# Attention stage: the small group of a projection tile moved in front of the value products, a large one between the turns, the gating product moved to their middle

## The chip, the cores and the metric

The kernel runs as one program on one core of a Trainium2 chip. The metric is the time of one execution on the device in microseconds (us), lower is better. The engines of the core are PE (TensorE, with its weight loads shown as PEld), DVE (VectorE), ACT (ScalarE), POOL (GpSimd) and SP (SyncE, which here only issues transfers).

## The reference, cut to what matters

One encoder layer over 1280 tokens (a prompt of 256 and a sample of 1024), width 1024. The part that the change touches:

```
xn = rms_norm(x, norm_mix_g)
q, k, v, gu, gv, z, xbc, dt, gates = split(xn @ w_in)
# A: banded attention, blocks of 128 queries against 3 x 128 keys, 8 heads
scores = qn @ kn.T + bias;  pr = exp(scores - m) / denom;  y_a = pr @ v
# B: chunked gating over 128 positions, 4 groups
vn = layer_norm(gelu(gv));  sv = w_spatial @ vn + b;  y_b = gelu(gu) * sv
```

After it come the state space branch (C), the merge of the three branches with the output projection, and the feed-forward part.

## The kernel before

Everything is held transposed, features on the 128 partitions and tokens along the free axis. The program has stages with a barrier between them: `project`, `attention_and_gmlp`, `state_space`, `merge` with the feed-forward part. The order on each engine is written out by hand, and engines wait for each other on counting semaphores.

`attention_and_gmlp` works on 10 chunks of 128 tokens. In each of its 10 steps (`step`, chunks 0 to 9) it does for its chunk the attention values and the gating branch, for the next chunk the scores, and beside them one tile of the late part of the input projection, which fills TensorE's time. Such a tile (`LateTiles`, name `la`) is 128 output features by 1280 tokens, in three token groups with an index g of 0 to 2. A group is 8 x 3 matmuls (`three_products`, L155 to L157: each weight and each activation is split into a high and a low half). Their widths come from

```
GROUPS = ((0, 512), (512, 512), (1024, 256))
```

so a group is "large" (512 tokens) or "small" (256). The accumulators alternate between two banks of `la_acc`; `read_out` on ScalarE (L780) copies each to `la_result`, with SiLU in chunks 0 to 5 and plainly in chunks 6 to 9, and the tile is stored from SP's queue (L742).

In a step TensorE's order is: `scores` of the next chunk (four pairs of L974 into two banks of `ps_scores`, two slices of group 0 behind each pair); `turn_v` (L1020, the gating branch's values are transposed); group 1 in one piece; `values`: eight turns (L985, three 128 x 128 transposes of the probabilities each, into two banks of `ps_turned`), which ScalarE copies out (L1161, `probs_T`), and four `products` (L994) of two heads each, with two slices of group 2 ahead of each product; at the end `mix` (L1026, the gating product of 4 x 128 columns).

ScalarE's order in a step is: `high_half` of a weight tile (L195), `gm_sum` (L1170), `read_out` of group 0, `gm_square` (L1174), `gm_root` (L1179, a square root), `read_out` of group 1, `results` (8 x L1161, then L1166), `read_out` of group 2, `exponents` of the next chunk (L1153). Before SiLU, the square root and the exponential the compiler puts an ACT_TABLE_LOAD, where the table before was another's.

VectorE's order is: `add_bias` (L1064, empties `ps_scores`), `low_half` (L200), `gm_mean`, `divide` (L1090 gives the probabilities, one operation a head), `gm_inverse` (L1101), `maxima` of the next chunk, `gm_normal` (L1106, gives `vn`, for which `mix` waits), `gm_gate` (L1113, L1116, which wait for `mix`). Turn i waits for probability i and, from the third on, for the copy of the turn two before it.

Of the kernel before, what the change touches and what calls it, by code (L numbers as in the profile page):

```python
# [25 lines left out]
HEADS, HD = 8, 64  # L26
# [32 lines left out]
GROUPS = ((0, 512), (512, 512), (1024, 256))  # L59
# [658 lines left out]
class LateTiles:  # L718
# [1 line left out]

    def __init__(self, ctx, nc, sem, name, ws, scratch, xn, first):
        def sb(what, shape):
            return ctx.enter_context(nc.sbuf_tensor(f"{name}_{what}", shape, F32))

        self.ws, self.result = ws, sb("result", [P, 2, T])
        self.acc = ctx.enter_context(nc.psum_tensor(f"{name}_acc", [P, 2, 512], F32))
        self.out = scratch["late_T"]
        self.xn, self.first = xn, first  # L730
        self.stored = [sem(f"{name}_stored{s}") for s in range(2)]
        self.full, self.read = (sem(f"{name}_{w}") for w in ("full", "read"))

# [26 lines left out]

    def product(self, pe, s, m, g, ks=range(KD)):

        t0, n = GROUPS[g]
        if 0 in ks:
            if g == 0:
                pe.wait_ge(self.ws.split_done, m + (B_LATE + self.first + 1))
            if not (isinstance(m, int) and 3 * m + g < 2):
                pe.wait_ge(self.read, m * 3 + (g - 1))
        for k in ks:
            mm = three_products(pe, self.acc[:, (s + g) % 2, 0:n], self.ws.hi[:, s, k], self.ws.lo[:, s, k],  # L770
                                self.xn[0][:, k, t0:t0 + n], self.xn[1][:, k, t0:t0 + n], k == 0, k == KD - 1)
        if KD - 1 in ks:
            mm.then_inc(self.full, 1)

    def read_out(self, act, s, m, g, func=ACT.Identity):
        t0, n = GROUPS[g]
        if g == 0 and not (isinstance(m, int) and m < 2):
            act.wait_ge(self.stored[s], m * 8 - 8 * s)
        act.wait_ge(self.full, m * 3 + (g + 1))
        act.activation(self.result[:, s, t0:t0 + n], self.acc[:, (s + g) % 2, 0:n], func).then_inc(self.read, 1)  # L780
# [66 lines left out]
def attention_and_gmlp(nc, a, scratch, consts, ws, xn, bias, sem):  # L847
# [9 lines left out]
    with ExitStack() as ctx:  # L857
# [19 lines left out]
        waste = sb("gm_waste", [P, E])  # L877
        gm_stat = sb("gm_stat", [P, 2, 4])
        y = sb("gm_y", [P, 2, G, P])
        late = LateTiles(ctx, nc, sem, "la", ws, scratch, xn, 0)  # L880
        ps_s = ctx.enter_context(nc.psum_tensor("ps_scores", [P, 2, 512], F32))
        ps_t = ctx.enter_context(nc.psum_tensor("ps_turned", [P, 2, 512], F32))
        ps_o = ctx.enter_context(nc.psum_tensor("ps_out", [P, 512], F32))
# [19 lines left out]
        with nc.Block() as block:  # L903
# [60 lines left out]
            @block.tensor  # L964
            def _(pe):
                def scores(s, chunk, loads, between=lambda h: None):

                    pe.wait_ge(qk_in[s], loads)
                    for j in range(HEADS // 2):
                        if not (first(chunk) and j == 0):  # L970
                            pe.wait_ge(s_read, chunk * 8 + 2 * j)
                        for g in range(2):
                            rows_of = slice(g * HD, (g + 1) * HD)
                            pe.matmul(ps_s[:, g, 0:W], q[rows_of, s, j, :], k[rows_of, s, :],  # L974
                                      start=True, stop=True).then_inc(s_full, 1)
                        between(2 * j)
                        between(2 * j + 1)

                def values(s, chunk, loads, between):
                    def turn(i):  # L980
                        pe.wait_ge(p_ready, chunk * 8 + (i + 1))
                        if not (first(chunk) and i < 2):
                            pe.wait_ge(t_read, chunk * 8 + (i - 1))
                        for b in range(3):
                            mm = pe.transpose(ps_t[:, i % 2, b * P:(b + 1) * P], S[:, s, ORDER[i], b * P:(b + 1) * P],  # L985
                                              masks[:, IDENT])
                        mm.then_inc(t_full, 1)

                    def products(j):

                        pe.wait_ge(t_read, chunk * 8 + (2 * j + 2))
                        for b in range(3):
                            for g in range(2):
                                mm = pe.matmul(ps_o[g * HD:(g + 1) * HD, j * P:(j + 1) * P],  # L994
                                               v[:, s, b, g * HD:(g + 1) * HD], PT[:, (2 * j + g) % 4, b],
                                               start=b == 0, stop=b == 2)
                        return mm

                    turn(0)
                    turn(1)  # L1000
                    pe.wait_ge(v_in[s], loads)
                    if not first(chunk):
                        pe.wait_ge(o_read, chunk)
                    for j in range(HEADS // 2):
                        if j + 1 < HEADS // 2:
                            turn(2 * j + 2)
                            turn(2 * j + 3)
                        between(2 * j)
                        between(2 * j + 1)
                        mm = products(j)  # L1010
                    mm.then_inc(o_full, 1)

                def turn_v(s, chunk, loads):
                    pe.wait_ge(uv_in[s], loads)
                    if first(chunk):
                        pe.wait_ge(shift_ok, 1)
                    else:
                        pe.wait_ge(scaled, chunk * 4)
                    for j in range(G):
                        mm = pe.transpose(ps_g[:, j * P:(j + 1) * P], uv[:, s, G + j], masks[:, IDENT])  # L1020
                    mm.then_inc(turned, 1)

                def mix(s, chunk):
                    pe.wait_ge(vn, chunk + 1)
                    for g in range(G):
                        mm = pe.matmul(ps_g[:, g * P:(g + 1) * P], vt[:, s, g * P:(g + 1) * P], w_sT[:, g],  # L1026
                                       start=True, stop=True)
                    mm.then_inc(mixed, 1)

                def step(s, chunk, loads, ahead):  # L1030

                    if ahead is not None:
                        scores(1 - s, chunk + 1, ahead, lambda h: late.product(pe, s, chunk + 2, 0, [h]))
                    else:
                        late.product(pe, s, chunk + 2, 0)
                    turn_v(s, chunk, loads)
                    late.product(pe, s, chunk + 2, 1)
                    values(s, chunk, loads, lambda h: late.product(pe, s, chunk + 2, 2, [h]))
                    mix(s, chunk)

                late.product(pe, 0, 0, 0)
                scores(0, 0, 48)
                pe.wait_ge(small_in, 64)
                for g in range(G):
                    mm = pe.matmul(ps_g[:, g * P:(g + 1) * P], ln_b[:, g * P:(g + 1) * P], w_sT[:, g], start=True, stop=True)
                mm.then_inc(shifted, 1)
                for m, g in ((0, 1), (0, 2), (1, 0), (1, 1), (1, 2)):
                    late.product(pe, m, m, g)
                step(0, 0, 16, 48)
                step(1, 1, 16, 96)  # L1050
                with pe.Fori(1, NT // 2 - 1) as pair:
                    step(0, pair * 2, pair * 16 + 16, pair * 48 + 48)
                    step(1, pair * 2 + 1, pair * 16 + 16, pair * 48 + 96)
                step(0, NT - 2, 16 * NT // 2, 48 * NT // 2)
                step(1, NT - 1, 16 * NT // 2, None)
# [93 lines left out]
            def _(act):  # L1149
# [4 lines left out]
                                       accum_out=stat[:, s, 2, h:h + 1]).then_inc(exp_done, 1)  # L1154
                    act.activation(stat[:, s, 1], stat[:, s, 1], ACT.Exp).then_inc(exp_done, 1)

                def results(s, chunk, stores):
                    for h in range(HEADS):

                        act.wait_ge(t_full, chunk * 8 + (h + 1))  # L1160
                        act.activation(PT[:, h % 4].rearrange("p b q -> p (b q)"), ps_t[:, h % 2, 0:W],  # L1161
                                       ACT.Identity).then_inc(t_read, 1)
                    act.wait_ge(o_full, chunk + 1)
                    if stores is not None:
                        act.wait_ge(o_stored[s], stores)
                    act.activation(out[:, s].rearrange("p j q -> p (j q)"), ps_o[:], ACT.Identity).then_inc(o_read, 1)  # L1166
# [14 lines left out]
                def step(s, chunk, stores, more=True, func=ACT.Silu):  # L1181
# [3 lines left out]
                    late.read_out(act, s, chunk + 2, 0, func)  # L1185
                    gm_square(s, chunk)
                    gm_root(s, chunk)
                    late.read_out(act, s, chunk + 2, 1, func)
                    results(s, chunk, stores)
                    late.read_out(act, s, chunk + 2, 2, func)  # L1190
                    if more:
                        exponents(1 - s, chunk + 1)
# [919 lines left out]
```

## Time and profile before

| | us |
|---|---|
| median of three runs | 2490.12 (2489.49 to 2491.94) |
| the profiled execution, its own time | 2490.52 |
| its span, first to last instruction | 2488.7 |
| TensorE busy in the span | 2367.1 |
| attention stage, from its first to its last matmul | 476.92 to 793.0 |

The span is 1.8 us shorter than the profiled execution's own time; that is what lies around it. Busy time of TensorE is the sum of its matmuls, whose ends are modelled. A row of the timeline begins with the start and the duration; in square brackets stands how long the engine was idle ahead of it, and what ended that. The granted clock (PEclk) is a share of TensorE's full clock of 2.4 GHz: 1.00 is 2.4 GHz and 0.50 is 1.2 GHz.

### The profile page before, as it was taken

To read this page: it belongs to the slowest core of one execution; us is meant where nothing else is said; L and a number is where in the kernel's file an instruction comes from. 1 tells how busy PE (TensorE), PEld (TensorE's weight loads), DVE (VectorE), ACT (ScalarE), POOL (GpSimd) and SP (SyncE) were. 2 spreads that over 40 slices of the span, in tenths; PEclk is the share of its full clock that TensorE was granted. 3 is DMA by queue.
4 is the path that set the end of the run, shared out by engine and by line. 5 is a ranking of instruction groups with operands and counts; after the bars stand their busy time and mean duration, and the time that the engine had idled before them with its cause. 6 is when DMAs were issued, how large, how long until landed. Compare 5 with 4: busy or idle time off the path is not lost.

```text
span 2488.7 us, 33412 instructions
## 1 busy us (share of the span) xinstructions
PE 2367.1 (95%) x13062; PEld 1970.9 (79%) x13062; DVE 1103.9 (44%) x1581; ACT 857.8 (34%) x1543; POOL 155.5 (6%) x72
## 2 busy tenths in 40 slices
PE   3999999699998999999799999999999999999999
PEld 1778888576777888888678888788888888888887
DVE  4310265336553666677555453533333333333333
ACT  4331223246654544566544131421121212111120
POOL 3333343000000000000000000000000000000000
PEclk8999999899999999999899999999999999999999
DMA  3122223422233666788574341111111111111112
GB/s 121 39 85 76 78 89 124 139 93 94 93 105 112 185 199 200 236 242 250 173 260 137 96 155 38 35 35 43 35 42 34 42 34 42 34 42 34 42 34 93
DMA packets 171003, 251.09 MB, mean 101 GB/s; under 512 B 10883, under 2 KB 125827, under 8 KB 168236
## 3 DMA queue, kind: packets, MB, share of 16 engines
q1 hardware_dynamic: 170924, 250.01, 31.8%
q8 instruction: 53, 0.87, 0.1%
q14 instruction: 26, 0.21, 0.0%
HBM read 189.57 MB, written 62.50 MB: 101 GB/s over the span
## 4 chain that ended last, share of the span: by engine, by line
PE 49%; DVE 1%; DMA 0%; SPq 0%; ACT 0%; issue 0%; DVEq 0%
PE acc L155 16%; PE acc L156 16%; PE acc L157 16%; DVE r_lo L1672 1%; DMA merged<-s_y_T 0%; PE acc L1929 0%; SPq L1709 0%; ACT r_hi L1662 0%; DVE h_T L1880 0%; DVE r_lo L1670 0%; ACT gates L1854 0%; DVE sums L1793 0%; DVE sums L1867 0%; DVE merged L1796 0%; DVE h_T L2036 0%
## 5 line engine op out<-in xcount | busy, mean ns | idle before, releaser
L155 PE MATMUL acc<-r_hi,w_hi 128*128 128x512 f32 (+1 forms) x1344 | 478.2, 356 | 17.1 <-DVE r_lo L1670 17.1
L156 PE MATMUL acc<-r_hi,w_lo 128*128 128x512 f32 (+1 forms) x1344 | 477.3, 355 | 0.0
L157 PE MATMUL acc<-r_lo,w_hi 128*128 128x512 f32 (+1 forms) x1344 | 476.5, 355 | 0.0
L155 PEld LDWEIGHTS acc<-r_hi,w_hi 128*128 128x128 f32 x1344 | 255.2, 190 | 54.8 <-issue 14.4
L156 PEld LDWEIGHTS acc<-r_hi,w_lo 128*128 128x128 f32 x1344 | 255.2, 190 | 35.3
L157 PEld LDWEIGHTS acc<-r_lo,w_hi 128*128 128x128 f32 x1344 | 254.8, 190 | 35.7
L156 PE MATMUL acc<-u_hi,w_lo 128*128 128x512 f32 (+1 forms) x768 | 273.6, 356 | 0.0
L155 PE MATMUL acc<-u_hi,w_hi 128*128 128x512 f32 (+1 forms) x768 | 273.6, 356 | 0.0
L157 PE MATMUL acc<-u_lo,w_hi 128*128 128x512 f32 (+1 forms) x768 | 273.6, 356 | 0.0
L195 ACT ACTIVATE w_hi<-w_raw 128x1024 fp32r<-128x1024 f32 x119 | 124.9, 1050 | 386.2 <-PE acc L157 380.1
L155 PE MATMUL acc<-xn_hi,w_hi 128*128 128x512 f32 (+1 forms) x624 | 225.2, 361 | 13.5 <-DVE xn_lo L317 8.7
L2036 DVE TENSOR_TENSOR h_T<-h_T,acc 128x512 f32<-128x512 f32 (+1 forms) x192 | 114.9, 598 | 264.8 <-PE acc L157 264.8
L156 PE MATMUL acc<-xn_hi,w_lo 128*128 128x512 f32 (+1 forms) x624 | 223.0, 357 | 0.0
L157 PE MATMUL acc<-xn_lo,w_hi 128*128 128x512 f32 (+1 forms) x624 | 222.5, 357 | 0.0
L200 DVE TENSOR_TENSOR w_lo<-w_raw,w_hi 128x1024 fp32r<-128x1024 f32 x119 | 145.5, 1223 | 99.0 <-ACT w_hi L195 98.9
L155 PE MATMUL s_l_acc<-xn_hi,w_hi 128*128 128x512 f32 (+1 forms) x480 | 179.8, 375 | 8.0 <-PEq L111 6.1
L157 PE MATMUL s_l_acc<-xn_lo,w_hi 128*128 128x512 f32 (+1 forms) x480 | 172.2, 359 | 0.0
L156 PE MATMUL s_l_acc<-xn_hi,w_lo 128*128 128x512 f32 (+1 forms) x480 | 171.7, 358 | 0.0
L155 PEld LDWEIGHTS acc<-u_hi,w_hi 128*128 128x128 f32 x768 | 144.1, 188 | 23.5
L156 PEld LDWEIGHTS acc<-u_hi,w_lo 128*128 128x128 f32 x768 | 144.1, 188 | 23.5
L157 PEld LDWEIGHTS acc<-u_lo,w_hi 128*128 128x128 f32 x768 | 144.1, 188 | 23.4
L1994 ACT ACTIVATE u_hi<-gates 128x512 fp32r<-128x512 f32 (+1 forms) x96 | 54.0, 562 | 312.8 <-DVE gates L2024 312.8
(204 smaller groups left out, 3458.0 us busy)
## 6 DMA issues: line engine op xcount, KB each, us to landing
w_raw<-in_w_tiles SPq DMA_DIRECT2D x146, 512.0 KB, 3.7
c_w<-s_ac SPq DMA_DIRECT2D x20, 1024.0 KB, 4.6
c_xbc<-s_xbc_T SPq DMA_DIRECT2D x20, 768.0 KB, 4.7
s_late_T<-s_l_result SPq DMA_DIRECT2D x20, 640.0 KB, 6.9
c_grown<-s_grown SPq DMA_DIRECT2D x40, 256.0 KB, 6.0
gates<-s_late_T SPq DMA_DIRECT2D x16, 512.0 KB, 3.8
s_xbc_T<-x_T_sb SPq DMA_DIRECT2D x12, 640.0 KB, 3.2
s_late_T<-la_result SPq DMA_DIRECT2D x12, 640.0 KB, 3.6
```

What stands on the lines that cost most here:

```text
L155: pe.matmul(out, w_hi, x_hi, start=first, stop=False)
L156: pe.matmul(out, w_lo, x_hi, start=False, stop=False)
L157: return pe.matmul(out, w_hi, x_lo, start=False, stop=last)
L195: act.activation(self.hi[:, s], self.raw[:, s], ACT.Identity).then_inc(self.hi_done, 1)
L200: dve.tensor_tensor(self.lo[:, s], self.raw[:, s], self.hi[:, s].bitcast(F32), ALU.subtract).then_inc(self.split_done, 1)
L1672: dve.scalar_tensor_tensor(low, src, self.gain[:, k:k + 1], high.bitcast(F32), ALU.mult, ALU.subtract).then_inc(self.low, 1)
L1994: act.activation(self.u_hi[:, i, t0:t0 + n], self.relu[:, u % 2, 0:n], ACT.Square).then_inc(self.high, 1)
L2036: dve.tensor_tensor(hh, hh, self.acc2[:, g, 0:n], ALU.add).then_inc(self.added, 1)
```

## The change

The tiles of this stage get their groups in another order: large, small, large. Group 1, which runs in one piece in front of the values, is the small one now, and group 2, which is spread between the turns, is a large one. `mix` moves from the end of the step to behind the second product of the values. On ScalarE `read_out` of group 1 moves from in front of the eight copies to their middle. The stage of the state space branch keeps the old order of groups for its own tiles. Nothing is added or taken away.

```
-    def __init__(self, ctx, nc, sem, name, ws, scratch, xn, first):
+    def __init__(self, ctx, nc, sem, name, ws, scratch, xn, first, groups=GROUPS):
...
-        t0, n = GROUPS[g]
+        t0, n = self.groups[g]
...
-        late = LateTiles(ctx, nc, sem, "la", ws, scratch, xn, 0)
+        late = LateTiles(ctx, nc, sem, "la", ws, scratch, xn, 0, (GROUPS[0], GROUPS[2], GROUPS[1]))
...
                         between(2 * j)
                         between(2 * j + 1)
                         mm = products(j)
+                        if j == 1:
+                            middle()
...
-                    values(s, chunk, loads, lambda h: late.product(pe, s, chunk + 2, 2, [h]))
-                    mix(s, chunk)
+                    values(s, chunk, loads, lambda h: late.product(pe, s, chunk + 2, 2, [h]), lambda: mix(s, chunk))
...
                     for h in range(HEADS):
-
+                        if h == HEADS // 2:
+                            middle()
...
-                    late.read_out(act, s, chunk + 2, 1, func)
-                    results(s, chunk, stores)
+                    results(s, chunk, stores, lambda: late.read_out(act, s, chunk + 2, 1, func))
```

The order of TensorE's instructions around the first turns of chunk 0, before. These are the end of group 1, the first four turns (`ps_turned`), the first slices of group 2 and the first product:

```order
L157 MATMUL la_acc<-xn_lo,w_hi 128x512
L985 MATMUL ps_turned<-masks_sb,scores_sb 128x128 x12
L155 MATMUL la_acc<-xn_hi,w_hi 128x256
L156 MATMUL la_acc<-xn_hi,w_lo 128x256
L157 MATMUL la_acc<-xn_lo,w_hi 128x256
```

The same place now:

```order
L157 MATMUL la_acc<-xn_lo,w_hi 128x256
L985 MATMUL ps_turned<-masks_sb,scores_sb 128x128 x12
L155 MATMUL la_acc<-xn_hi,w_hi 128x512
L156 MATMUL la_acc<-xn_hi,w_lo 128x512
L157 MATMUL la_acc<-xn_lo,w_hi 128x512
```

The group ahead of the turns is the narrow one now, and the slices behind them are wide.

The end of chunk 0's step on TensorE before, from the last slices of group 2 to the first scores of the next step:

```order
L155 MATMUL la_acc<-xn_hi,w_hi 128x256
L156 MATMUL la_acc<-xn_hi,w_lo 128x256
L157 MATMUL la_acc<-xn_lo,w_hi 128x256
L994 MATMUL ps_out<-probs_T,v_sb 64x128 x6
L1026 MATMUL ps_gmlp<-w_sT,v_turned_sb 128x128 x4
L974 MATMUL ps_scores<-k_sb,q_sb 128x384 x2
```

Now `mix` (L1028 in the new numbering, `ps_gmlp`) stands in the middle of the values, behind the second product and ahead of the last turns:

```order
L994 MATMUL ps_out<-probs_T,v_sb 64x128 x6
L1028 MATMUL ps_gmlp<-w_sT,v_turned_sb 128x128 x4
L985 MATMUL ps_turned<-masks_sb,scores_sb 128x128 x6
L155 MATMUL la_acc<-xn_hi,w_hi 128x512
L156 MATMUL la_acc<-xn_hi,w_lo 128x512
L157 MATMUL la_acc<-xn_lo,w_hi 128x512
```

The step now ends with a product, and the next scores follow it at once.

ScalarE in chunk 1's step before, from the load of SiLU's table for group 0 to the end of the step:

```order
L780 ACT_TABLE_LOAD
L780 ACTIVATE la_result<-la_acc 128x512
L1174 ACTIVATE gm_waste,gm_stat<-v_turned_sb,gm_stat 128x512
L1179 ACT_TABLE_LOAD
L1179 ACTIVATE gm_stat<-gm_stat 128x1
L780 ACT_TABLE_LOAD
L780 ACTIVATE la_result<-la_acc 128x512
L1161 ACTIVATE probs_T<-ps_turned 128x384 x8
L1166 ACTIVATE attn_out<-ps_out 128x512
L780 ACTIVATE la_result<-la_acc 128x256
```

And now, from the square root on:

```order
L1181 ACT_TABLE_LOAD
L1181 ACTIVATE gm_stat<-gm_stat 128x1
L1163 ACTIVATE probs_T<-ps_turned 128x384 x4
L780 ACT_TABLE_LOAD
L780 ACTIVATE la_result<-la_acc 128x256
L1163 ACTIVATE probs_T<-ps_turned 128x384 x4
L1168 ACTIVATE attn_out<-ps_out 128x512
L780 ACTIVATE la_result<-la_acc 128x512
```

The copies of the turns (`probs_T`) begin right behind the square root, and the table load with the copy of group 1 comes after four of them. The number of table loads is the same.

## Rows read from the trace of the kernel before

**Rows 1.** The page, busy time of each engine and share of the span.
```profile
PE 2367.1 (95%) x13062; PEld 1970.9 (79%) x13062; DVE 1103.9 (44%) x1581; ACT 857.8 (34%) x1543; POOL 155.5 (6%) x72
```

**Rows 2.** What TensorE waited for from 540 to 775: us, times, longest.
```profile
PE ps_turned L985 <- ACT probs_T L1161: 7.2, 8, 1.1
PE ps_scores L974 <- DVE scores_sb L1064: 4.0, 8, 0.5
```

**Rows 3.** Timeline of TensorE in chunk 3's step.
```profile
604.63 0.92 PE L974 MATMUL ps_scores<-k_sb,q_sb 64*128 64x384 f32 x4
...
607.68 0.92 PE L974 MATMUL ps_scores<-k_sb,q_sb 64*128 64x384 f32 x4 [0.55 <-DVE scores_sb L1064]
...
615.23 0.48 PE L155 MATMUL la_acc<-xn_hi,w_hi 128*128 128x512 f32 x1
...
620.80 0.82 PE L985 MATMUL ps_turned<-masks_sb,scores_sb 128*128 128x128 f32 x6
622.76 0.91 PE L985 MATMUL ps_turned<-masks_sb,scores_sb 128*128 128x128 f32 x6 [1.14 <-ACT probs_T L1161]
...
631.47 1.16 PE L1026 MATMUL ps_gmlp<-w_sT,v_turned_sb 128*128 128x128 f32 x8
632.56 0.92 PE L974 MATMUL ps_scores<-k_sb,q_sb 64*128 64x384 f32 x4
```

**Rows 4.** Timeline of ScalarE in chunk 3's step.
```profile
615.51 0.60 ACT L1170 ACTIVATE v_turned_sb<-ps_gmlp 128x512 f32<-128x512 f32 x1 [3.62 <-PE ps_gmlp L1020]
...
620.12 0.20 ACT L1179 ACTIVATE gm_stat<-gm_stat 128x1 f32<-128x1 f32 x1
...
622.13 0.87 ACT L1161 ACTIVATE probs_T<-ps_turned 128x384 f32<-128x384 f32 x2
```

**Rows 5.** Timeline of TensorE, small group of tile 1, first scores of chunk 0's step.
```profile
519.05 0.28 PE L155 MATMUL la_acc<-xn_hi,w_hi 128*128 128x256 f32 x1
...
522.02 0.92 PE L974 MATMUL ps_scores<-k_sb,q_sb 64*128 64x384 f32 x4
...
524.45 0.92 PE L974 MATMUL ps_scores<-k_sb,q_sb 64*128 64x384 f32 x4
```

**Rows 6.** Timeline of VectorE in chunk 3's step.
```profile
604.84 1.13 DVE L1113 SCALAR_TENSOR_TENSOR gm_y<-ps_gmlp,ln_g_sb,shift 128x128 f32<-128x128 f32 x4 [7.24 <-PE ps_gmlp L1026]
...
616.78 2.73 DVE L1090 TENSOR_SCALAR scores_sb<-scores_sb,softmax_stat 128x384 f32<-128x384 f32 x8
...
624.99 0.54 DVE L1106 TENSOR_SCALAR v_turned_sb<-v_turned_sb,gm_stat 128x512 f32<-128x512 f32 x1
```

**Rows 7.** Timeline of ScalarE in chunk 6's step.
```profile
703.51 0.20 ACT L1179 ACTIVATE gm_stat<-gm_stat 128x1 f32<-128x1 f32 x1 [1.11 <-DVE gm_stat L1101]
...
705.20 0.87 ACT L1161 ACTIVATE probs_T<-ps_turned 128x384 f32<-128x384 f32 x2
```

**Rows 8.** Timeline of ScalarE and TensorE in chunk 9's step, the last.
```profile
777.15 0.58 ACT L1170 ACTIVATE v_turned_sb<-ps_gmlp 128x512 f32<-128x512 f32 x1
...
782.52 0.86 ACT L1161 ACTIVATE probs_T<-ps_turned 128x384 f32<-128x384 f32 x2
...
783.15 0.90 PE L985 MATMUL ps_turned<-masks_sb,scores_sb 128*128 128x128 f32 x6 [0.94 <-ACT probs_T L1161]
```

**Rows 9.** Timeline of TensorE, three longer gaps elsewhere.
```profile
505.35 0.77 PE L155 MATMUL la_acc<-xn_hi,w_hi 128*128 128x512 f32 x1 [3.05 <-ACT la_result L780]
...
820.52 0.39 PE L155 MATMUL s_l_acc<-xn_hi,w_hi 128*128 128x256 f32 x1 [1.86 <-ACT s_l_result L780]
...
1473.86 0.47 PE L155 MATMUL acc<-r_hi,w_hi 128*128 128x512 f32 x1 [1.73 <-DVE r_lo L1670]
```

**Rows 10.** Windows: busy us of PE, PEld, DVE, ACT, POOL, then PEclk, DMA share, GB/s.
```profile
820.00:822.00 2.00, 1.48 (x11) 1.49 (x12) 1.99 (x2) 2.00 (x4) 0.00 (x0) 0.94 0.00 0
822.00:824.00 2.00, 2.00 (x12) 2.00 (x11) 2.00 (x3) 2.00 (x8) 0.00 (x0) 0.50 0.00 0
824.00:826.00 2.00, 1.22 (x9) 0.93 (x10) 1.77 (x2) 2.00 (x8) 0.00 (x0) 0.71 0.01 4
...
1472.00:1474.00 2.00, 0.27 (x3) 0.17 (x2) 1.74 (x4) 2.00 (x5) 0.00 (x0) 1.00 1.04 422
```

More of the change, by code:

```diff
@@ L729, in __init__ @@
         self.out = scratch["late_T"]
-        self.xn, self.first = xn, first
+        self.xn, self.first, self.groups = xn, first, groups
         self.stored = [sem(f"{name}_stored{s}") for s in range(2)]
@@ L775, in read_out @@
     def read_out(self, act, s, m, g, func=ACT.Identity):
-        t0, n = GROUPS[g]
+        t0, n = self.groups[g]
         if g == 0 and not (isinstance(m, int) and m < 2):
@@ L977, in scores, with values @@
                         between(2 * j + 1)
-                def values(s, chunk, loads, between):
+                def values(s, chunk, loads, between, middle):
                     def turn(i):
@@ L1155, in exponents, with results @@
                     act.activation(stat[:, s, 1], stat[:, s, 1], ACT.Exp).then_inc(exp_done, 1)
-                def results(s, chunk, stores):
+                def results(s, chunk, stores, middle):
                     for h in range(HEADS):
+                        if h == HEADS // 2:
+                            middle()
                         act.wait_ge(t_full, chunk * 8 + (h + 1))
```

## The prediction, made before the changed kernel ran

> **What bounds the kernel now.** I read the page first: TensorE is busy for 2367.1 of 2488.7 us [rows 1], no other engine for half. So time comes or goes only where TensorE waits, or where its clock falls. Then I asked what TensorE waits for in the steps of the attention stage, where all edits lie. Between 540 and 775, in eight steps, there are two waits a step: the third turn waits for ScalarE's copy of the first (7.2 us in all), and the second pair of scores waits for VectorE to empty the banks (4.0 us) [rows 2]. The edits move work around both. Last I read one step on each engine in its own timeline, to see what comes last at each wait.
>
> The turn wait, in chunk 3's step: group 1 runs from 615.23 to 620.80, the first two turns follow, the third starts at 622.76 after 1.14 us of idling [rows 3]. It is released by the copy that starts at 622.13, 0.63 us before. Ahead of this copy ScalarE has a chain: it begins at 615.51, when `turn_v` is done (ScalarE had waited 3.62 us for it), and has its square root at 620.12 [rows 4]. Then come a table load and the copy of group 1, and only then the copies of the turns. So the copies hang on `turn_v` and on ScalarE's own chain, and not on how long group 1 takes.
>
> The scores wait: `gm_gate` on VectorE waits for `mix`, the last thing of the step, so it starts at 604.84 [rows 6], after the next scores have begun at 604.63, and the bias addition queues behind it. The second pair starts 3.05 us after the first, with 0.55 of idling [rows 3]. In chunk 0's step, where no gating stands ahead of the addition, it is 2.43 us [rows 5].
>
> **The change part by part.** The matmuls are the same in number and shape, so only waits and clock can differ.
>
> *Mix in the middle.* It waits for `vn`, ready at 624.99 + 0.54 = 625.53 [rows 6]. From the third turn at 622.76 to `mix` at 631.47 there are four rounds of turns, slices and product [rows 3], 2.2 us each. In the new order `mix` stands behind two of them, each longer by 6/24 of a large group's excess over a small one (2.60 us, below), 0.65 us. With the third turn at 620.86 (below) it is reached at 620.86 + 4.4 + 1.3 = 626.6. That leaves 1.0 us of slack, so I cost this wait at nothing; the cover is VectorE having done `maxima` by then, and each us by which `vn` came later than that would be a us a step. Behind `mix` TensorE's last turns are queued, and they would carry any wait. `gm_gate` then runs during the last turns, and VectorE is free at the next scores: 3.05 - 2.43 = 0.6 us saved at each of eight steps (chunks 1 to 8), **-4.7 us** (the idle row says 4.0, the rest is the modelled ends). `mix` itself (631.47 to 632.56, 1.09 us) moves at its own price.
>
> *The small group in front.* A small group takes 522.02 - 519.05 = 2.97 us [rows 5], the large one 620.80 - 615.23 = 5.57 [rows 3]. The first turns come 2.60 us earlier, at 618.20. The probabilities exist by then (eight take 2.73 us from 616.78 on [rows 6], 0.34 each). But the third turn comes no earlier than its copy allows.
>
> *Copy of group 1 in the middle of the copies.* The copies now follow the square root, whose row is 0.20 long; I put them 0.1 us behind its start: at 620.23 in place of 622.13, 1.90 us earlier [rows 4]. The third turn follows at 620.86. TensorE's idling there grows by 2.60 - 1.90 = 0.70 us, from 1.14 to 1.84. Six steps with SiLU (chunks 0 to 5): **+4.2 us**. The table load and copy of group 1 now fall where ScalarE waited for turns anyway (the slices between the turns are 0.65 us longer a round besides), so they delay nothing. In chunks 6 to 8 there is no table load: square root at 703.51, copies at 705.20 [rows 7], so they gain only 705.20 - 703.62 = 1.58 us. Idling grows by 1.02, from the 0.50 that the sum of rows 2 leaves for them (7.2 - 5 x 1.14 = 1.5 for three) to 1.5: **+3.1 us**.
>
> *The last step.* Chunk 9's has no scores, so ScalarE is late: its chain starts at 777.15 without having waited [rows 8], behind the exponents, which come behind the last product's copy. Before, `mix` stood between that product and the next step; now it doesn't, so ScalarE starts up to 1.09 us later against TensorE (I take 0.9), and 0.2 more for a read-out that is 512 wide in place of 256 (a 512-wide one takes 0.58 [rows 8]; an estimate). The copies come 1.1 later and 0.5 earlier (no 512-wide read-out stands between them and the square root), the first turns want to be 2.60 earlier: idling grows by 2.60 + 1.1 - 0.5 = **+3.2 us**, from 0.94 to 4.1, in two pieces, since the first turn now has to wait for its probabilities too.
>
> *Start and end.* In the prologue TensorE waits 3.05 us until ScalarE has copied group 1 of the first tile [rows 9], which is now small: -0.2. At the end the store of the gating result is no longer last, but the last read-out is wider and follows TensorE's end directly: I put it at +0.2, and take 1 us either way for the bounds. Transfers are the same, each some us earlier or later, and nothing in the step waits for one. Sum of waits: 4.2 + 3.1 + 3.2 - 4.7 = **+5.8 us**.
>
> *The clock.* It is 1.00 through all ten steps now. A gap of 1.86 us at 820.52 [rows 9] was followed, about 1.2 us into the next matmuls, by a fall to 0.50; from the three windows it lasted 0.24 + 2.0 + 1.16 = 3.4 us [rows 10]. A gap of 1.73 at 1473.86 [rows 9] left it at 1.00 [rows 10]. So gaps of this size sometimes cost the clock, and the new gap of 1.84 us lies between these two, with turns on both sides, which are short matmuls. Nothing in the trace fixes the odds; bounds are none of ten and all of ten. I take every second of five steps at 1.84, one in three of the four at 1.5, and the last step surely (its gap is longer than the 3.05 that went with a fall): 2.5 + 1.3 + 1 = 4.8 falls. A fall of 3.4 us at half speed costs at most 1.7 us; I take 1.4, since some of it is idling or short matmuls. **+6.7 us**, with 0 and 17 as bounds.
>
> The Trainium skill (page "TensorE: Matmul & The Clock Gate", section "Why this matters for your kernels") warns only of gaps longer than any that I expect in chunks 0 to 8. By this rule the waits alone would count, up to the last step; the row at 820.52 speaks against it, the one at 1473.86 for it. The rival below has its price.
>
> Together +12.5 us on the profiled execution's 2490.5, which stands 0.4 above the median of 2490.1: 2503.0 on the one base, 2502.6 on the other, and I say **2503 us**.
>
> **The rivals.**
> - *The waits as worked out, no falls of the clock in the steps.* For it: the present gaps of 1.14 never cost it, and 1.73 didn't. Against: 1.86 did. 2490.1 + 5.8 = 2495.9, up to 2497.3 with the last step's fall. The skill's rule above ends here. 22 in 100.
> - *A fall in nearly every step.* From the first turn to the slices behind the fourth there would be 0.8 + 1.84 + 0.9 us [rows 3], some 3.5 us of turns and idling only; if turns do not keep the clock up, this stretch is longer than the gap of 3.05. Against: the present stretch, 0.7 shorter, goes with no fall in any of ten steps. 2490.1 + 5.8 + 10 x 1.5 = 2511. The skill states, on the same page in "Part 4: PE-mode transpose", that transposes do not count as matmuls do for the clock; no row here tests it alone. 10 in 100.
> - *No net change.* The turn wait grows by less, say 0.2 in place of 0.7, because something in ScalarE's chain also shortens when group 0's read-out or VectorE's `gm_inverse` comes sooner, and the last step loses 2: 2490.1 - 4.7 + 2 + 2 = 2489.4. Against: the chain is back to back from 615.51. 12 in 100.
> - *Faster.* One mechanism: the copies of the turns start as much earlier as the turns do, so that the turn wait does not grow at all and only the scores' gain is left. It decides from 2.6 us on, that is from copies before 619.5 in chunk 3's step. 2490.1 - 4.7 = 2485.4, or some 2484 if the last step gains as well. Against: the square root stands ahead of them at 620.12. 5 in 100.
>
> My forecast (waits, and about half of the possible falls; 2498 to 2508) has 51 in 100.
>
> **How the numbers follow.** A measurement of this kernel tells 0.2%, 5 us, from no change. Faster is the last rival. Within 0.2%, up to 2495.1, are the third and a third of the first, some 0.2 in all. The rest is slower. The range leaves out most of the third rival and the upper half of the second: 2494 to 2510.
>
> **What would show it.** In the new profile: the third turn idles 1.8 us in chunks 1 to 5, 1.5 in chunks 0 and 6 to 8, and over 3 in the last; the second scores pair does not idle in chunks 1 to 8; nothing waits at `mix`; the granted clock falls below 1.00 in about four or five of the ten steps. It would be wrong if the copies started well before the square root's place, if `mix` waited for `vn`, or if the clock stayed up through gaps of 1.8 us.

## The result and the profile after

The change makes the kernel slower: 2501.11 us (median of six runs, 2499.11 to 2501.55) against 2490.3 for the kernel before beside it (six runs, 2489.49 to 2491.94). The ratio is 1.0041, with a 95% interval of 1.003 to 1.0053, so +10.8 us where +12.9 were forecast. The profiled execution took 2501.0 us with a span of 2499.2; before it was 2490.52 and 2488.7.

The page of the kernel after, busy time of each engine, answers to [rows 1]:

```profile
PE 2369.8 (95%) x13062; PEld 1968.2 (79%) x13062; DVE 1104.7 (44%) x1581; ACT 857.7 (34%) x1543; POOL 155.5 (6%) x72
```

TensorE is busy for only 2.7 us more; most of the other 8 us are waiting. What TensorE waited for, first from 540 to 775 (answers to [rows 2]), then from 520 to 812, with the last step and the end of the stage:

```profile
PE ps_turned L985 <- ACT probs_T L1163: 13.8, 8, 1.9
```
```profile
PE ps_turned L985 <- ACT probs_T L1163: 17.7, 10, 2.4
PE s_l_acc L155 <- PEq L111: 7.2, 1, 7.2
PE ps_turned L985 <- DVE scores_sb L1091: 1.6, 1, 1.6
```

The wait of the scores has gone without a trace. The wait of the third turn has nearly doubled, 7.2 to 13.8 us in eight steps, and nothing waits at `mix`. The timeline of TensorE in chunk 2's step shows the new order (compare [rows 3]):

```profile
576.61 0.92 PE L974 MATMUL ps_scores<-k_sb,q_sb 64*128 64x384 f32 x4
...
579.05 0.92 PE L974 MATMUL ps_scores<-k_sb,q_sb 64*128 64x384 f32 x4
...
586.59 0.36 PE L155 MATMUL la_acc<-xn_hi,w_hi 128*128 128x256 f32 x1
...
589.53 0.82 PE L985 MATMUL ps_turned<-masks_sb,scores_sb 128*128 128x128 f32 x6
592.20 0.90 PE L985 MATMUL ps_turned<-masks_sb,scores_sb 128*128 128x128 f32 x6 [1.85 <-ACT probs_T L1163]
...
598.24 1.16 PE L1028 MATMUL ps_gmlp<-w_sT,v_turned_sb 128*128 128x128 f32 x8
...
604.58 0.92 PE L974 MATMUL ps_scores<-k_sb,q_sb 64*128 64x384 f32 x4
```

The second pair of scores starts 2.44 us after the first, as it did in chunk 0's step before [rows 5]. The first turns start 2.94 us behind the small group's begin, and then TensorE idles 1.85 us. The same step on ScalarE (compare [rows 4]):

```profile
586.87 0.60 ACT L1172 ACTIVATE v_turned_sb<-ps_gmlp 128x512 f32<-128x512 f32 x1 [1.79 <-PE ps_gmlp L1022]
...
591.48 0.20 ACT L1181 ACTIVATE gm_stat<-gm_stat 128x1 f32<-128x1 f32 x1
591.59 0.85 ACT L1163 ACTIVATE probs_T<-ps_turned 128x384 f32<-128x384 f32 x2
593.65 1.28 ACT L780 ACT_TABLE_LOAD   x1
594.95 0.38 ACT L780 ACTIVATE la_result<-la_acc 128x256 f32<-128x256 f32 x1
595.82 0.88 ACT L1163 ACTIVATE probs_T<-ps_turned 128x384 f32<-128x384 f32 x2 [0.49 <-PE ps_turned L985]
```

The chain starts as soon as `turn_v` is done, the square root comes 4.61 us later (before 4.61 too), the first copy 0.11 behind it, and the third turn 0.61 after that. The table load now lies where ScalarE would wait for turns: even behind it and the copy of group 1, ScalarE waits 0.49 us for the next turn. On VectorE `vn` is ready at 596.90 and `mix` takes it at 598.24, 1.3 us later:

```profile
596.36 0.54 DVE L1107 TENSOR_SCALAR v_turned_sb<-v_turned_sb,gm_stat 128x512 f32<-128x512 f32 x1
599.54 1.13 DVE L1114 SCALAR_TENSOR_TENSOR gm_y<-ps_gmlp,ln_g_sb,shift 128x128 f32<-128x128 f32 x4 [2.63 <-PE ps_gmlp L1028]
```

The last step and the end of the stage, on TensorE and on SP's queue (compare [rows 8]):

```profile
783.56 0.88 PE L985 MATMUL ps_turned<-masks_sb,scores_sb 128*128 128x128 f32 x6 [1.56 <-DVE scores_sb L1091]
...
786.83 1.51 PE L985 MATMUL ps_turned<-masks_sb,scores_sb 128*128 128x128 f32 x6 [2.39 <-ACT probs_T L1163]
...
802.74 0.43 SPq L742 DMA_DIRECT2D s_late_T<-la_result  x1
803.53 0.38 SPq L926 DMA_DIRECT2D s_y_T<-gm_y  x1
...
808.76 0.77 PE L155 MATMUL s_l_acc<-xn_hi,w_hi 128*128 128x512 f32 x1 [7.18 <-PEq L111]
```

The windows show the granted clock (the number behind the last x; columns as in [rows 10]):

```profile
619.00:621.00 2.00, 0.83 (x7) 0.79 (x8) 1.97 (x4) 1.67 (x5) 0.00 (x0) 1.00 0.00 0
621.00:623.00 2.00, 2.00 (x7) 1.31 (x5) 2.00 (x1) 1.97 (x4) 0.00 (x0) 0.57 0.00 0
623.00:625.00 2.00, 2.00 (x15) 1.39 (x15) 1.75 (x5) 0.30 (x1) 0.00 (x0) 0.58 0.00 0
625.00:627.00 2.00, 2.00 (x14) 1.46 (x12) 0.00 (x0) 0.87 (x2) 0.00 (x0) 1.00 0.00 0
...
785.00:787.00 2.00, 0.17 (x1) 0.20 (x2) 1.58 (x6) 0.90 (x3) 0.00 (x0) 0.53 0.00 0
787.00:789.00 2.00, 2.00 (x9) 1.81 (x9) 0.00 (x0) 1.18 (x4) 0.00 (x0) 0.50 0.00 0
789.00:791.00 2.00, 2.00 (x7) 1.16 (x7) 0.00 (x0) 0.15 (x1) 0.00 (x0) 0.50 0.00 0
```

In this execution the clock fell from 2.4 to 1.2 GHz twice in the ten steps: behind the 1.85 us gap of chunk 3's step, and in the last step, where it was low from about 785 to 792. Chunks 1, 2, 4 and 5 had gaps of the same length and no fall. The fall in the last step began inside its gap of 2.39 us, 1.7 us ahead of the third turn.

Where the 10.5 us between the two profiled executions lie, from the starts of the stages and of the steps (the first scores of each):

| | us |
|---|---|
| ahead of the stage (its first matmul at 477.52, before 476.92) | +0.6 |
| first matmul to first scores (43.52, before 45.10) | -1.6 |
| the steps of chunks 0 to 8, waits | +2.5 |
| chunk 3's fall of the clock (29.52 against its neighbours' 27.97) | +1.55 |
| last step (28.53, before 23.04): idling +3.0, clock about +2.5 | +5.5 |
| end: last matmul to the next stage (7.26, before 6.20) | +1.1 |
| behind the stage | +0.9 |
| sum, against 2499.2 - 2488.7 = 10.5 | +10.55 |

### The profile page after: what moved, and what is told of

It is laid out like the page before. It is cut to its first block and busy times, and to the rows that moved or that the text cites. A ratio compares the mean times of both kernels' runs of the same rounds, so it can differ in the third digit from the quotient of the medians.

```text
span 2499.2 us, 33412 instructions
## 1 busy us (share of the span) xinstructions
PE 2369.8 (95%) x13062; PEld 1968.2 (79%) x13062; DVE 1104.7 (44%) x1581; ACT 857.7 (34%) x1543; POOL 155.5 (6%) x72
```

## The experiments

In each case the ratio is to the kernel before, run beside it on the same chip (2491.19 us for the first four kernels, 2490.5 for the next four, 2491.55 for the last). Theory A is mine: the copies of the turns hang on ScalarE's chain, so whatever stands ahead of the turns only decides how long TensorE idles, and falls of the clock come on top. Its rivals are named where they differ.

### The change in its parts

**Regrouping alone.** The kernel after, but with `mix` at the step's end and the copy of group 1 ahead of the eight copies, as before.

```
-  values(s, chunk, loads, ..., lambda: mix(s, chunk))
+  values(s, chunk, loads, ..., lambda: None)
+  mix(s, chunk)
...
-  results(s, chunk, stores, lambda: late.read_out(act, s, chunk + 2, 1, func))
+  late.read_out(act, s, chunk + 2, 1, func)
+  results(s, chunk, stores, lambda: None)
```

> Only the order of the token groups is changed (large, small, large); mix stays at the end of the step and the copy of group 1 in front of the eight copies. Theory: the copies of the turns hang on ScalarE's chain behind turn_v, so the first turns come 2.6 us earlier and the third no earlier. Its idling should grow from 1.14 to about 3.5 us in chunks 1 to 5, from 0.50 to about 1.8 in chunks 6 to 8 and from 0.94 to about 3.5 in the last; the scores pair idles its 0.5 us as before. That is 14 + 4 + 2.6 = 21 us of waits, and gaps of 3.5 us should bring a fall of the clock in nearly every one of chunks 0 to 5, 1.5 us each, +9: about 2520 us. Rival: the chain moves with the turns, or the turns are slowed by something else than the copies; then the regrouping alone costs no more than it does in the changed kernel, up to 2505 us.

Measured: 2526.69 us (2525.35 to 2528.48), ratio 1.0139 [1.0123, 1.0154]. Waits of TensorE from 520 to 850 (the stage ends later here), chunk 1's third turn, and the window behind it:

```profile
PE ps_turned L985 <- ACT probs_T L1164: 28.9, 10, 3.5
```
```profile
571.61 1.51 PE L985 MATMUL ps_turned<-masks_sb,scores_sb 128*128 128x128 f32 x6 [3.55 <-ACT probs_T L1164]
```
```profile
571.00:574.00 3.00, 2.39 (x9) 2.23 (x10) 2.90 (x4) 1.83 (x5) 0.00 (x0) 0.50 0.00 0
```

The third turn idles 3.5 us in chunks 1 to 5 and 3.2 in chunk 0, that is 2.4 more than before, of the 2.6 us by which the small group is shorter: the turns came earlier and their copies did not. In chunks 6 to 8 it idles 1.8 us, only 1.3 more than the 0.5 before. There ScalarE's copy of group 1 had been waiting for TensorE to finish that group, so the copies of the turns hung on TensorE too, as chunk 6's step of the kernel before shows:

```profile
704.70 0.60 ACT L780 ACTIVATE la_result<-la_acc 128x512 f32<-128x512 f32 x1 [0.99 <-PE la_acc L157]
```

The clock fell in every one of the six steps of chunks 0 to 5, and in the last. The waits of the turns grew by 20.6 us in the profiled execution (2528.48 us); some 15 us more lie with the seven falls, where the expectation had 9. Three of the falls, in chunks 1, 3 and 5, lasted 6.8 us and the others 3.4.

**Mix alone.** The old groups, only `mix` in the middle.

```
-  late = LateTiles(..., xn, 0, (GROUPS[0], GROUPS[2], GROUPS[1]))
+  late = LateTiles(..., xn, 0)
...
-  results(s, chunk, stores, lambda: late.read_out(act, s, chunk + 2, 1, func))
+  late.read_out(act, s, chunk + 2, 1, func)
+  results(s, chunk, stores, lambda: None)
```

> Only mix moves to the middle of the values; groups and the copy of group 1 as before. Theory: the idling of the second scores pair (0.5 us in chunks 1 to 8) goes and nothing waits at mix, -4.7 us; in the last step ScalarE starts 0.9 us later against TensorE, which its third turn shows, +0.9: 2490.3 - 3.8 = 2486.5 us. Rival: mix in the middle waits for vn or delays the turns behind it, and takes back what the scores give: 2490 us or more, with a wait in front of mix in the trace.

Measured: 2487.66 us (2484.0 to 2489.44), ratio 0.9985 [0.9976, 0.9994]. The scores wait is gone, nothing waits at `mix`, and the third turn idles 1.14 us in chunks 1 to 5 as before. The last step and the end of the stage lose, though:

```profile
778.33 0.90 PE L985 MATMUL ps_turned<-masks_sb,scores_sb 128*128 128x128 f32 x6 [1.83 <-ACT probs_T L1163]
795.25 0.77 PE L155 MATMUL s_l_acc<-xn_hi,w_hi 128*128 128x512 f32 x1 [7.20 <-PEq L111]
```

The third turn of the last step idles 1.83 us (before 0.94), and the wait for the next stage is 7.20 us (before 6.13). A step of chunks 1 to 5 is about 0.7 us shorter than before, so the move gains some 5.8 us in chunks 0 to 8 and gives 2 back behind them.

**The copy of group 1 alone.** The old groups, `mix` at the end, `read_out` of group 1 in the middle of the copies.

```
-  late = LateTiles(..., xn, 0, (GROUPS[0], GROUPS[2], GROUPS[1]))
+  late = LateTiles(..., xn, 0)
...
-  values(s, chunk, loads, ..., lambda: mix(s, chunk))
+  values(s, chunk, loads, ..., lambda: None)
+  mix(s, chunk)
```

> Only the copy of group 1 moves to the middle of the eight copies; groups and mix as before. Theory: the copies are free 1.9 us earlier and then hang on the turns themselves. A copy starts 0.6 us after its turn and takes 0.5, so the third turn still idles about 0.4 us: from 1.14 to 0.4 in chunks 1 to 5, from 0.77 to 0.4 in chunk 0, little in chunks 6 to 8 (0.50 to 0.4), 0.5 in the last. Sum -5 us: 2485.4 us. Rival: the table load of SiLU in the middle of the copies delays the later turns or products by 1.3 us a step in chunks 0 to 5, +8: 2493 us, with idling at the fifth turn.

Measured: 2485.41 us (2483.83 to 2487.88), ratio 0.9976 [0.9966, 0.9986]. Waits of TensorE from 520 to 812:

```profile
PE ps_scores L974 <- DVE scores_sb L1066: 4.0, 8, 0.5
PE ps_turned L985 <- ACT probs_T L1164: 3.6, 10, 0.5
```

The scores' 4.0 us stand as in [rows 2]; the third turn idles 0.34 us in every step and 0.46 in the last. It is not zero, because the third turn can't come sooner than its copy, and that waits for the first turn itself: this is the floor of two banks with nothing to do between their first and second use.

**Both, without the regrouping.**

```
-  late = LateTiles(..., xn, 0, (GROUPS[0], GROUPS[2], GROUPS[1]))
+  late = LateTiles(..., xn, 0)
```

> Mix and the copy of group 1 as in the changed kernel, groups in the old order (large, large, small). Theory: both gains add, -3.8 - 5 = -9 us: 2481.5 us, and the clock stays at 1.00 through the steps, since the longest gap in a step is 0.4 us up to the last step's 1.4. Against the changed kernel (2501.1) it is then the regrouping that costs 20 us. Rival: the two interact (the mixed step is as long as the longest of its chains), and only one of the gains shows: 2485 to 2487 us.

Measured: 2481.13 us (2480.03 to 2482.8), ratio 0.996 [0.9946, 0.9973]. The waits from 520 to 812:

```profile
PE ps_turned L985 <- ACT probs_T L1163: 4.4, 10, 1.3
```

The granted clock is 1.00 in all steps. Two of the three parts of the change gain, 3.5 and 5.8 us alone and 10.1 together; the regrouping costs 20.0 us on top of them (2501.11 - 2481.13) and 35.5 by itself. A step takes 26.35 us against 27.97.

### The clock

**The gap filled.** The kernel after, and in the gap five matmuls of 512 columns that compute nothing that is kept (the first product overwrites their bank). The rival says that the falls have another cause than the gap, such as the turns.

```
   if j == 0:
       for _ in range(5):
           pe.matmul(ps_o[:], late.ws.hi[:, s, 0], xn[0][:, 0, 0:512], start=True, stop=True)
```

> The changed kernel, and in every step five matmuls of 512 columns more, whose result is written over by the products, in the gap ahead of the third turn. They do no needed work and take 1.15 us of a gap of 1.5 to 1.85 us. Theory: the waits stay (the third turn starts where it did, idle 0.7 or less), the clock does not fall in chunks 0 to 8, and what the one fall of the profiled run cost there (1.5 us), with part of the last step's 2.3, is saved: 2498.5 us, at least 1.5 below the changed kernel. Rival: the falls do not come from the gap; then one or two stay and the time is 2501 us or above.

Measured: 2498.36 us (2495.32 to 2500.17), ratio 1.0028 [1.0018, 1.0038]. Chunk 3's third turn and its window:

```profile
618.81 1.42 PE L1007 MATMUL ps_out<-xn_hi,w_hi 128*128 128x512 f32 x5
620.90 0.90 PE L985 MATMUL ps_turned<-masks_sb,scores_sb 128*128 128x128 f32 x6 [0.68 <-ACT probs_T L1166]
```
```profile
620.00:622.00 2.00, 1.32 (x10) 1.01 (x9) 1.97 (x3) 1.67 (x6) 0.00 (x0) 1.00 0.00 0
```

The third turn still comes when its copy allows, the steps are as long as after (27.97), and none of the ten had a fall, the last one, idling in two pieces of 1.56 and 1.24 us, included. So the falls go with the gaps: the turns by themselves bring none. Whether turns beside an empty gap add to the odds is not shown, since the filler parts the turns as well. The falls are worth 2.8 us by the medians, and 4.0 by the rows of the profile of after.

**The last step as before.** The kernel after, with the last step's groups, `mix` and copy in the old order.

```
+  def group_of(self, m, g):
+      return (GROUPS if isinstance(m, int) and m == NT + 1 else self.groups)[g]
...
+  last = ahead is None
+  values(..., lambda: None if last else mix(s, chunk))
+  if last:
+      mix(s, chunk)
...
+  if not more:
+      late.read_out(act, s, chunk + 2, 1, func)
+  results(s, chunk, stores, lambda: late.read_out(...) if more else None)
```

> The changed kernel, but the last chunk's step as before: its tile in the old order of groups, mix at the end, the copy of group 1 ahead of the eight copies. Theory: of the last step's 5.5 us about 1.1 stay, since ScalarE still comes late out of step 8, and with an idling of 2.0 us the clock may or may not fall: 2501.1 - 3.5 = 2497.6 us. Rival: the last step's loss comes from what the steps before leave behind (ScalarE's lateness alone), and stays: 2500 us or above.

Measured: 2498.47 us (2490.46 to 2499.48), ratio 1.0024 [1.0014, 1.0035]. The last step's third turn idles 2.04 us, not 0.94, and the end of the stage is 6.13 us, as before. Two windows, behind the third turns of chunks 1 and 3:

```profile
563.00:566.00 3.00, 1.95 (x9) 1.72 (x10) 2.97 (x3) 2.61 (x7) 0.00 (x0) 0.78 0.00 0
...
623.00:626.00 3.00, 3.00 (x16) 1.87 (x15) 2.90 (x5) 1.62 (x2) 0.00 (x0) 0.50 0.00 0
```

In this execution chunk 1 fell as well as chunk 3, and the last step fell even with a gap of 2.04. One of the eight runs took 2490.46 us, 6 us less than the next, at a mean granted clock of 0.983 where the others had 0.978 to 0.980; what it was spared no profile shows. By the rows the last step idles 1.9 us less and the end of the stage is 1.1 shorter, 3.0 together; the medians show 2.6.

### Placement

**Slices ahead of the turns.** The kernel after; the two slices of group 2 of each round stand ahead of the pair of turns and not behind it, and so fill the gap with work that has to be done. The rival says that the copies would come later too, since they queue on the turns.

```
   for j in range(HEADS // 2):
+      between(2 * j)
+      between(2 * j + 1)
       turn(2 * j + 2); turn(2 * j + 3)
-      between(2 * j)
-      between(2 * j + 1)
       mm = products(j)
```

> The changed kernel with the two slices of group 2 ahead of each pair of turns in place of behind it, so that six wide matmuls (1.45 us) stand in the gap ahead of the third turn. Theory: the regrouping costs only because that gap is empty; the third turn should idle about 0.3 us in chunks 1 to 5 and nothing in 0 and 6 to 8, one us in the last: 1.45 + 5 x 1.5 + 3 x 1.5 + 1.4 = -15 us, and no fall of the clock in chunks 0 to 8, -1.5: 2484.5 us. Rival: the products, which now follow the turns at once, wait for copies, or the small group in front costs by itself: 2492 us or more.

Measured: 2485.2 us (2484.61 to 2487.05), ratio 0.9979 [0.997, 0.9988]. Chunk 3's third turn, and the new wait at `mix`:

```profile
617.40 0.90 PE L985 MATMUL ps_turned<-masks_sb,scores_sb 128*128 128x128 f32 x6 [0.44 <-ACT probs_T L1163]
```
```profile
PE ps_gmlp L1028 <- DVE v_turned_sb L1107: 1.2, 4, 0.3
```

The time falls by 16 us with the small group still in front, so most of the regrouping's loss was the empty gap. What is left is 4 us against the kernel with both parts and the old groups. But that kernel gains from the same placing too, as the next experiment shows: with the slices first in both, the old groups are 10 us faster (2475.2), 0.86 us a step and the rest in and behind the last step, where that kernel also keeps `mix` at the end. So the grouping still costs. In chunks 1 to 5 0.44 us of the 0.86 are the wait above; the rest is in no recorded wait and stays open. A step takes 26.67 us, and the clock stays at 1.00. The slack of `mix`, 1.3 us after, is used up in chunks 0 and 6 to 8.

**Both ideas on the old groups.** The kernel with `mix` and the copy in the middle and the old groups, its slices ahead of the turns, and `mix` at the end in the last step only.

> Groups in the old order, mix and the copy of group 1 in the middle (2481.1 us), with the two slices ahead of each pair of turns and, in the last step alone, mix at the end. Theory: the 0.34 us ahead of the third turn go in nine steps, -3.1, and the last step's 1.34 nearly all, -1.3: 2476.7 us. Rival: without the slices behind them the turns expose a wait of the products for the copies, 0.3 us at each of three products a step: 2485 us.

Measured: 2475.2 us (2472.98 to 2476.13), ratio 0.9935 [0.9921, 0.9948]. All that TensorE waits for on ScalarE's copies from 520 to 800:

```profile
PE ps_turned L985 <- ACT probs_T L1167: 0.6, 1, 0.6
```

There is no wait in chunks 0 to 8, a step takes 25.81 us, and the kernel is 15 us below the one before and 26 below the one after.

### The end of the stage

**The store of the gating result first.** The kernel after; in the last two steps this store is issued ahead of the other two.

```
+  if not loads:
+      store_y(s, chunk)
   store_out(s, chunk)
   ...
-  store_y(s, chunk)
+  if loads:
+      store_y(s, chunk)
```

> The changed kernel, with the store of the gating result ahead of the other two stores on SP's queue in the last two steps. Theory: the 1.1 us that the end of the stage became longer (from the last product's end to the first matmul of the next stage 7.26 us, before 6.20) come from this store, which was issued last, behind a late store that is no earlier: with it out of the way the end takes some 6.3 us, -1 us: 2500 us. Rival: the late tile's store alone sets the end, and it stays 7.2 us. The steps have the same gaps as in the changed kernel, so it also shows again how many of them cost the clock: by the theory one to four of nine, and not always the same ones.

Measured: 2501.29 us (2499.28 to 2502.22), ratio 1.0037 [1.0023, 1.005]; after was 1.0041. The medians can't tell it; the trace can (SP's queue, and the next stage's first matmul):

```profile
798.82 0.38 SPq L926 DMA_DIRECT2D s_y_T<-gm_y  x1
...
803.56 0.35 SPq L742 DMA_DIRECT2D s_late_T<-la_result  x1
...
808.44 0.77 PE L155 MATMUL s_l_acc<-xn_hi,w_hi 128*128 128x512 f32 x1 [6.29 <-PEq L111]
```

TensorE idles 6.29 us ahead of the next stage in place of 7.18. The store of the gating result, which SP had queued 0.8 us behind that of the late tile, landed 4.1 us after its issue; as the first it takes 2.3. So putting it first gives back 0.9 of the 1.1 us at the end.

What brought the 1.1 us is `mix`, and not the wider last group. The wait for the next stage is 7.2 us in every kernel whose last step has `mix` in the middle and the stores in the old order, with the old groups too (7.20 with `mix` alone), and 6.1 to 6.2 in every kernel that has it at the end, with the wide last group too (6.12 with the regrouping alone). At the end `mix` takes 1.09 us of this wait as work; moved to the middle it leaves it empty. In chunks 0 to 8 of this execution the clock fell once, in chunk 3, and once more in the last step.

## Why the prediction came out right, step by step

**What holds the copies: right, and shown.** The copies start 0.11 us behind the square root's start (0.1 said), and the third turn 0.61 us after that (0.63). The kernel with the regrouping alone shows the rule from the other side: 2.6 us less in front of the turns, and 2.4 more idling in chunks 0 to 5. For chunks 6 to 8 the reading "not on how long group 1 takes" was wrong for the kernel before, where ScalarE waited 0.99 us for that group. It did no harm, since the term was worked out from the square root, behind which the copies of the changed kernel do start.

**The scores wait, -4.7 us: right.** It is gone in the two kernels with only `mix` or with `mix` and the copy in the middle too. In the changed kernel the turn waits of chunks 0 to 8 grew by 7.3 and the steps by 2.5 us, which leaves -4.8. Alone the move is worth 3.5 us by the medians, because the steps of chunks 0 to 8 gain some 5.8 there, and the last step (0.9) and the end of the stage (1.1) give 2 back.

**The turn wait, +4.2 and +3.1 us: right.** It reads 1.85 in chunks 1 to 5 (1.84 said) and 1.5 in chunks 0 and 6 to 8. The sum had chunk 0 go from 1.14 to 1.84, where it went from 0.77 to 1.48: the same growth of 0.7. The waits of chunks 0 to 8 together are +2.5 us where the terms sum to +2.6.

**`mix` waits for nothing: right**, with 1.3 us of slack where 1.0 was said. That it was a cover that could be used up is shown by the kernel with the slices first.

**The last step, +3.2 us: right in its waits** (3.95 us in two pieces against 0.94, so +3.0). What it waits for first is the probability, 1.56 us, as said. The parts by themselves bear out the terms: `mix` alone adds 0.9 us of idling in this step (0.9 said), the copy alone takes 0.5 off (0.5 said), the regrouping alone adds 2.4 (2.8 said, with the wider read-out).

**The clock, +6.7 us: mis-sized.** There were two falls and not 4.8: none in the gaps of 1.5, one in five of the gaps of 1.85. They cost 4.0 us by the rows (1.55 and some 2.5), since the last step's was low for about 7 us and not 3.4. "The clock stayed up through gaps of 1.8 us" stands in my list of signs of being wrong, and in four of five such gaps it did. Over the three executions with these gaps (after, the last step as before, the store first) the clock fell at 4 of 15 gaps of 1.85 us and at none of 12 of 1.5; with 3.2 to 3.6 it fell at 6 of 6. I had said one in two and one in three. The term was 2.7 us too large. That is more than the 2.0 us by which the working (+12.5) missed the profiled execution (+10.5); +0.6 ahead of the stage and +0.9 behind it, which no term had, make up for some of it. That the total came so near is in this part luck.

**Start and end, -0.2 and +0.2: mis-sized, and one of their reasons was wrong.** The prologue gained 1.6 us: its gap is 2.70 us in place of 3.05, and the stretch at half clock that goes with it was 3.4 us in place of 6.8, which I had not counted. This is chance and not the change: from the stage's first matmul to its first scores the six kernels with the new groups took 43.5 to 45.6 us, and the five with the old ones 43.8 to 45.7. The step "the store of the gating result is no longer last" was wrong: SP's order is written out too, and keeps that store behind the late tile's, which is issued 1.24 us after TensorE's last product now and was issued 0.07 after the last `mix`. What the sum missed is that `mix` no longer fills the wait at the end: +1.1 us, of which the kernel with the store first gets 0.9 back. The two errors nearly cancel (-0.5 against 0.0), which is luck too.

**The rivals.** The rule of the Trainium skill (page "TensorE: Matmul & The Clock Gate", section "Why this matters for your kernels"), by which gaps as long as these would cost nothing but themselves, held for most gaps in this kernel's steps, but 4 of the 15 of 1.85 us went with a fall: its case of 2496 didn't come, and the measurement decides against it. The case with a fall in nearly every step did not come either, and the filled gap shows that the turns alone do not bring a fall. "No net change" needed a turn wait that grows by 0.2 us a step; it grew by 0.7. "Faster" needed copies ahead of the square root, and they came behind it.

Open: what decides which of several equal gaps goes with a fall. Chunk 3 fell in all three executions and its neighbours once in twelve, which these runs do not explain. Length alone does not decide: in the next stage a gap of 1.86 to 1.94 us, the one at 820.52 of [rows 9], went with a fall in 10 of the 11 profiled executions (all but the kernel with both parts and the old groups), against 4 of 15 in the steps. Open too is the +0.9 us behind the stage. It goes with the regrouping: from the next stage's first matmul to the end of the span the six kernels with the new groups took 1690.4 to 1691.4 us, and the five with the old ones 1689.6 to 1690.0. Why is not shown.

## What to carry to other kernels

Filler work belongs in the gap, and only the chain that ends the wait says where the gap is. Making what stands ahead of a wait shorter lengthens the wait by nearly as much when the wait is set by another engine's own chain (35 us here, falls of the clock included). The same filler placed between the first and the second use of a bank took most of the wait away (1.85 to 0.44 us a step), and all of it with the old groups. Take a change of several parts apart before it is kept or dropped: two parts of this one gain 10 us, and the third takes 20. And look at the last iteration by itself: work that stands behind everything else there may be filling the wait for the next stage, as `mix` did, and the order of the last stores on their queue is worth 0.9 us here.

## What was not expected of the hardware

A gap of 1.85 us on TensorE went with a fall of the clock in 4 of 15 cases, one of 1.5 us in none of 12, one of 2.04 in the one case seen; while the last step with 1.56 and 1.24 us (the gap partly filled) had none. Two kernels add to this: the gaps of 1.8 us in chunks 6 to 8 with the regrouping alone, and the 1.83 us of the last step with `mix` alone, had none either.

The falls at the turns came in two lengths. In nine cases the clock fell between 0.3 us before TensorE's third turn and 1.4 us after it, and stayed low for 3.4 us. In five it fell 1.2 to 1.7 us before the third turn, inside the gap, and stayed low for 6.8 us: the last step of the changed kernel and of the one with the store first, and chunks 1, 3 and 5 with the regrouping alone. So a longer gap costs more than by its own length: it also goes with the longer fall.
